# The decay's logits as one product over 96 rows of hi and lo parts, in place of an fp32 product over 32 rows

## The reference

```python
xn = _rmsnorm(x, p['norm1_g'])
z = jnp.einsum('btd,de->bte', xn, p['w_in'])
rg_x, rg_y, q, k, v, g_lr, g_out, m_a, m_b = jnp.split(z, split_points, axis=-1)
...
zg = jnp.einsum('btr,rk->btk', g_lr, p['gla_w_gate']) + p['gla_b_gate']
log_alpha = (jax.nn.log_sigmoid(zg.astype(f32)) / GLA_TAU).reshape(B, T, GLA_HEADS, GLA_DK)
```

## Time and profile before

| | |
|---|---|
| median of 3 runs | 1923.3 us (1923.18 to 1924.96) |
| the profiled execution, its own time | 1920.77 us |
| its span, first to last instruction | 1919.0 us |
| TensorE busy | 1890.9 us, 99% |
| weight loads on TensorE busy | 1860.3 us, 97% |
| VectorE busy | 921.1 us, 48% |
| ScalarE busy | 565.7 us, 29% |
| mean granted TensorE clock | 0.996 |

### The profile page before, as it was taken

One profiled execution on the slowest core, in us unless ns is written; L12 is line 12 of the kernel. 1 busy time (PEld: TensorE's weight loads), 2 busy tenths in 40 slices (PEclk: granted clock), 3 DMA queues, 4 the chain that ended last, 5 costly groups with the idle time before them and its releaser, 6 DMA issues. The chain is left out here.

```text
span 1919.0 us, 28820 instructions
## 1 busy us (share of the span) xinstructions
PE 1890.9 (99%) x11866; PEld 1860.3 (97%) x11866; DVE 921.1 (48%) x1067; ACT 565.7 (29%) x630; POOL 27.6 (1%) x24
## 2 busy tenths in 40 slices
PE   7999999999999999999999999999999999999998
PEld 6999899999999999999999999999999999999997
DVE  6221377788754222422244455545453545455455
ACT  5010256755642111211132332222121212131225
POOL 0000000000000000000000000000000000000032
PEclk9999999999999999999999999999999999999999
DMA  5221132223111111311131111111111111111112
GB/s 196 97 76 52 37 110 104 93 79 134 63 61 44 55 44 44 133 44 47 51 133 44 56 45 46 53 45 45 45 45 44 55 45 45 44 44 50 44 58 89
DMA packets 48234, 126.72 MB, mean 66 GB/s; under 512 B 7000, under 2 KB 20184, under 8 KB 48144
## 3 DMA queue, kind: packets, MB, share of 16 engines
q1 hardware_dynamic: 27808, 87.97, 13.6%
q10 hardware_dynamic: 20352, 37.64, 5.6%
HBM read 107.71 MB, written 18.14 MB: 66 GB/s over the span
## 5 line engine op out<-in xcount | busy, mean ns | idle before, releaser
L417 PE MATMUL acc<-xn_hi,w_hi 128*128 128x346 f32 (+1 forms) x2496 | 814.6, 326 | 2.5 <-issue 2.2
L417 PE MATMUL acc<-xn_lo,w_hi 128*128 128x346 f32 (+1 forms) x2496 | 803.6, 322 | 0.0
L417 PE MATMUL acc<-xn_hi,w_lo 128*128 128x346 f32 (+1 forms) x2496 | 801.5, 321 | 0.0
L417 PEld LDWEIGHTS acc<-xn_hi,w_hi 128*128 128x128 f32 x2496 | 470.9, 189 | 6.2 <-issue 3.4
L417 PEld LDWEIGHTS acc<-xn_lo,w_hi 128*128 128x128 f32 x2496 | 472.4, 189 | 1.5
L417 PEld LDWEIGHTS acc<-xn_hi,w_lo 128*128 128x128 f32 x2496 | 471.0, 189 | 0.0
L795 ACT ACTIVATE w_hi<-w_raw 128x1024 fp32r<-128x1024 f32 x149 | 156.4, 1050 | 460.2 <-PE acc L417 459.1
L1196 DVE TENSOR_TENSOR w_lo<-w_raw,w_hi 128x1024 fp32r<-128x1024 f32 x149 | 182.4, 1224 | 182.0 <-ACT w_hi L795 181.9
L417 PE MATMUL acc<-act_hi,w_hi 128*128 128x344 f32 x504 | 161.7, 321 | 2.6 <-DVE residual L1610 2.6
L417 PE MATMUL acc<-act_hi,w_lo 128*128 128x344 f32 x504 | 161.6, 321 | 0.0
L417 PE MATMUL acc<-act_lo,w_hi 128*128 128x344 f32 x504 | 161.6, 321 | 0.0
(11 more groups left out here) (229 smaller groups left out, 2209.2 us busy)
## 6 DMA issues: line engine op xcount, KB each, us to landing
w_raw<-in_w SPq DMA_DIRECT2D x152, 512.0 KB, 3.5
ha_scratch<-rg_gelu_ha ACTq DMA_DIRECT2D x8, 519.0 KB, 2.7
h<-ha_scratch ACTq DMA_DIRECT2D x8, 519.0 KB, 6.1
residual<-in_x ACTq DMA_DIRECT2D x8, 519.0 KB, 6.4
gla_qk_pair<-qk_scratch ACTq DMA_DIRECT2D x8, 512.0 KB, 4.5
smp_v_rows<-smp_v_scratch ACTq DMA_DIRECT2D x8, 512.0 KB, 5.7
out_gla_sample<-smp_state ACTq DMA_DIRECT2D x8, 512.0 KB, 3.1
smp_state<-in_gla_state ACTq DMA_DIRECT2D x7, 512.0 KB, 4.9
```

The lines of the kernel that those rows point to most:

```text
L417: mm = nc.tensor.matmul(acc[g][:, n, 0:cw], w[s][:, t * P:(t + 1) * P], x[:, c0 + n * cw:c0 + (n + 1) * cw], start=a, stop=z)
```

## The change

The low rank and the gate weights get hi and lo parts like the wide operands, and the three terms are laid on 96 rows of one product: rows 0 to 31 hold hi by hi, rows 32 to 63 lo values by hi weights, rows 64 to 95 hi values by lo weights. For that the low rank's 32 weight columns are written three times (`low4`), so that its products give 96 rows; the lo part of the inputs now goes through the same 96 columns. `wg` is loaded six times instead of twice. After the scaling, which now signals `low_scaled`, five ScalarE copies and two VectorE subtractions make the fp32r parts, in place and in two tiles that are free then (`low_t`, `wg_t`). `low_ready` has to reach 2.

```diff
-            for r in (0, RANK):
+            for r in range(0, R6, RANK):
                 sp.dma_start(wg[r:r + RANK, :], I["gla_w_gate"]).then_inc(const_loaded, 16)
...
-                    nc.tensor.matmul(acc[0][0:R2, n, 0:NW], whi[0][:, R2 * k:R2 * (k + 1)], XH[:, c], start=k == 0, stop=False)
-                    mm = nc.tensor.matmul(acc[0][0:RANK, n, 0:NW], whi[0][:, R2 * k:R2 * k + RANK], XL[:, c],
-                                          start=False, stop=k == KB - 1)
+                    w = whi[0][:, R6 * k:R6 * (k + 1)]
+                    nc.tensor.matmul(acc[0][0:R6, n, 0:NW], w, XH[:, c], start=k == 0, stop=False)
+                    mm = nc.tensor.matmul(acc[0][0:R6, n, 0:NW], w, XL[:, c], start=False, stop=k == KB - 1)
...
-                    mm = nc.tensor.matmul(sb6[:, h * w:(h + 1) * w], wg[0:R2, h * DK:(h + 1) * DK],
-                                          glr[0:R2, bass.ds(c0, w)], start=True, stop=True)
+                    mm = nc.tensor.matmul(sb6[:, h * w:(h + 1) * w], wg_s[0:R6, h * DK:(h + 1) * DK],
+                                          glr_s[0:R6, bass.ds(c0, w)], start=True, stop=True)
...
-                pe.wait_ge(const_loaded, 16 * 6)
-                pe.wait_ge(low_ready, 1)
+                pe.wait_ge(const_loaded, 16 * 10)
+                pe.wait_ge(low_ready, 2)
...
-                    nc.scalar.activation(view3(glr[0:R2]), acc[0][0:R2, :, 0:NW], ACT.Copy).then_inc(acc_free[0], 1)
+                    nc.scalar.activation(view3(glr[0:R6]), acc[0][0:R6, :, 0:NW], ACT.Copy).then_inc(acc_free[0], 1)
...
+            act.wait_ge(const_loaded, 16 * 10)
+            nc.scalar.activation(wg_s[0:2 * R2], wg[0:2 * R2], ACT.Copy).then_inc(wg_hi_done, 1)
+            nc.scalar.activation(wg_t[2 * R2:R6], wg[2 * R2:R6], ACT.Copy).then_inc(wg_hi_done, 1)
+            act.wait_ge(low_scaled, 1)
+            for r in (0, 2 * R2):
+                nc.scalar.activation(glr_s[r:r + R2], glr[r:r + R2], ACT.Copy).then_inc(low_hi_done, 1)
+            nc.scalar.activation(low_t[R2:2 * R2], glr[R2:2 * R2], ACT.Copy).then_inc(low_hi_done, 1)
...
-            nc.vector.tensor_tensor(low3[:, :, RANK:R2], hd(raw[0], KB, RANK), low3[:, :, 0:RANK].bitcast(F32), ALU.subtract)\
+            low = hd(raw[0], KB, RANK).unsqueeze(2).broadcast_to([P, KB, 3, RANK])
+            nc.vector.tensor_tensor(low4[:, :, :, RANK:R2], low, low4[:, :, :, 0:RANK].bitcast(F32), ALU.subtract)\
...
-            nc.vector.tensor_tensor(glr[0:R2, :], glr[0:R2, :], rms[0:R2, :], ALU.mult).then_inc(low_ready, 1)
+            nc.vector.tensor_tensor(glr[0:R6, :], glr[0:R6, :], rms[0:R6, :], ALU.mult).then_inc(low_scaled, 1)
...
+            dve.wait_ge(wg_hi_done, 2)
+            nc.vector.tensor_tensor(wg_s[2 * R2:R6], wg[2 * R2:R6], wg_t[2 * R2:R6].bitcast(F32), ALU.subtract).then_inc(low_ready, 1)
+            dve.wait_ge(low_hi_done, 3)
+            nc.vector.tensor_tensor(glr_s[R2:2 * R2], glr[R2:2 * R2], low_t[R2:2 * R2].bitcast(F32), ALU.subtract).then_inc(low_ready, 1)
```

More of the change, by code:

```diff
@@ L53 @@
 R2 = 2 * RANK
+R6 = 3 * R2
 CH = 64
@@ L149, in build @@
         it = nxt("rg_i_b", C)
+        av_at = off[0]
         av = nxt("rg_a", C)
+        th_at = off[0]
         th = nxt("rg_mult", C)
@@ L167, in build @@
         rgtmp = at("rg_states_tmp", qkp_at + 1024, KB * NS)
-        glr = nxt("gla_low_rank", C)
+        glr_at = off[0]
+        glr, glr_s = nxt("gla_low_rank", C), at("gla_low_rank_split", glr_at, C, F32R)
         gw = nxt("rg_gate_weights", 2 * P)
@@ L172, in build @@
         svt = svb
-        wg = nxt("gla_gate_weights", QK)
+        wg_at = off[0]
+        wg, wg_s = nxt("gla_gate_weights", QK), at("gla_gate_weights_split", wg_at, QK, F32R)
         reset = nxt("scan_reset", 4 * PAIR, BF16, 2)
@@ L204, in build @@
         sq1 = (rt, it, av, th)
+        low_t, wg_t = at("gla_low_rank_hi", av_at, C, F32R), at("gla_gate_weights_hi", th_at, QK, F32R)
         act_bytes = (2 * GRP * CB + 31) // 32 * 32
@@ L268, in build @@
         V3 = V.rearrange("p (k c) -> p k c", k=KB)
-        low_ready = sem("low_ready")
+        low_scaled, low_hi_done, wg_hi_done, low_ready = (sem(n) for n in ("low_scaled", "low_hi_done", "wg_hi_done", "low_ready"))
         w_loaded, w_hi_done, w_split, unit_done = sems("w_loaded"), sems("w_hi_done"), sems("w_split"), sems("unit_done")
@@ L559, in zg_samples @@
                 for h in range(H):
-                    mm = nc.tensor.matmul(sb6[:, h * NS:(h + 1) * NS], wg[0:R2, h * DK:(h + 1) * DK],
-                                          glr[0:R2, NT:C], start=True, stop=True)
+                    mm = nc.tensor.matmul(sb6[:, h * NS:(h + 1) * NS], wg_s[0:R6, h * DK:(h + 1) * DK],
+                                          glr_s[0:R6, NT:C], start=True, stop=True)
                 mm.then_inc(zg_mm, 1)
@@ L620, in zg_pair @@
                     for h in range(H):
-                        mm = nc.tensor.matmul(sb6[:, h * PAIR:(h + 1) * PAIR], wg[0:R2, h * DK:(h + 1) * DK],
-                                              glr[0:R2, bass.ds(NMETA + PAIR * j, PAIR)], start=True, stop=True)
+                        mm = nc.tensor.matmul(sb6[:, h * PAIR:(h + 1) * PAIR], wg_s[0:R6, h * DK:(h + 1) * DK],
+                                              glr_s[0:R6, bass.ds(NMETA + PAIR * j, PAIR)], start=True, stop=True)
                     mm.then_inc(zg_mm, 1)
@@ L813, in _ @@
             act.preload_act_table_set(LN_EXP)
-            low3 = whi[0][:, 0:KB * R2].rearrange("p (k r) -> p k r", k=KB)
+            low4 = whi[0][:, 0:KB * R6].rearrange("p (k t r) -> p k t r", k=KB, t=3)
             act.wait_ge(w_loaded[0], 16)
-            nc.scalar.activation(low3[:, :, 0:RANK], hd(raw[0], KB, RANK), ACT.Copy).then_inc(w_hi_done[0], 1)
+            low = hd(raw[0], KB, RANK).unsqueeze(2).broadcast_to([P, KB, 3, RANK])
+            nc.scalar.activation(low4[:, :, :, 0:RANK], low, ACT.Copy).then_inc(w_hi_done[0], 1)
             act.wait_ge(prm_loaded, 16)
@@ L1314, in scores @@
             def scores(n, w):
-                dve.wait_ge(const_loaded, 16 * 6)
+                dve.wait_ge(const_loaded, 16 * 10)
                 dve.wait_ge(A_mm, n + 1)
```

## The result

The changed kernel takes 1927.2 us (median of 11 runs, 1926.6 to 1929.2) against 1923.0 us of the kernel before beside it (11 runs): ratio 1.0027, 95% interval 1.0017 to 1.0036. It is slower by 4 to 5 us, a little more than can be told from no change, where no change was forecast. The profiled execution took 1927.11 us, with a span 6.3 us longer than that of the earlier trace rows.

What follows compares the result with a forecast made beforehand. TensorE, busy for 99% of the span, was taken as the bound; -7.1 us of products, +4.6 wait and +2.5 low clock summed to 0.0, so 1923.3 us, no change, with a range of 1919.6 to 1927.4.

Steps and rivals of the forecast that it cites:

- products, pair blocks: TensorE, eight pair blocks in the passes: four instructions at 0.11 us, each block 0.44 instead of 1.17 us; 5.8 us saved.
- products, head and samples: TensorE, the head's and the samples' logits blocks: each 0.44 instead of 1.08 us; 1.3 us saved.
- wait before the first logits: TensorE idles until ScalarE's copies and VectorE's last subtraction finish: 4.6 us, bounds 4.4 and 5.1.
- low clock behind it: After the idle time before the first logits, wide products come at 0.29 instead of 0.16 us; 2.5 us lost.
- given back in the passes: Passes over token pairs, 225 to 520 us: no wait that could take the saved time back; 0 us.
- The step that failed: Passes, 225 to 520 us: TensorE busy throughout, so each removed instruction shortens the span by its pitch, with no wait behind.
- One reading beside it: Around the first logits: ScalarE's table load, its next work, began long after the copies would end, so nothing gets late.
- fp32 pace with the fall: Rival: narrow products at 0.22 us each, plus wait and low clock; +3.5 us, 1926.8 us, chance 0.18.
- The hidden wait: Rival: before the first logits copies overlap more or run ahead, so the wait hardly shows; -7.1 us, 1916.2 us, chance 0.07.
- the clock that doesn't fall: Rival: same wait before the first logits, products behind it still at 0.16 us; -2.5 us, 1920.8 us, chance 0.23.
- a new wait of TensorE inside the passes: Sign named as making the prediction wrong; it expected no TensorE wait from 225 to 520 us.

Runs made afterwards that it cites:

- after_warm: Changed kernel with 32 unread wide products on TensorE ahead of its wait for the logits' inputs; 1923.0 us, ratio 0.9999 to the kernel before.
- early_split: Changed kernel with five ScalarE copies behind the q and k loop's first turn, two VectorE subtractions ahead of its other three; 1917.7 us, ratio 0.9972.
- early_chain: early_split with VectorE masking scores before scaling the unit into rg_ext and copying the output before the weight's lo part; 1913.6 us, ratio 0.9958.
- after_again: The changed kernel once more, unaltered, for a second profile; 1926.3 us in one run.
- pairs_fp32: Changed kernel with the eight pair blocks as plain fp32 products over rows 0 to 31, without the lo terms; 1931.0 us, ratio 1.0045.
- before_chain: Kernel before, products unchanged, with VectorE's scores ahead of the scaling and output copies ahead of the lo part; 1921.4 us, ratio 0.9989.
- before_scores: Kernel before with only VectorE's masking of the scores moved ahead of the scaling into rg_ext; 1923.2 us, ratio 1.0007.

## Why the prediction was wrong

| term, us | forecast | from the trace after |
|---|---|---|
| products, pair blocks | -5.8 | -6.2 |
| products, head and samples | -1.3 | -1.4 |
| late before the wait | 0 | 0.2 |
| wait before the first logits | 4.6 | 5.3 |
| low clock behind it | 2.5 | 2.6 |
| longer low clock near 220 us | not seen | 2.6 |
| given back in the passes | 0 | 3.7 |
| behind the passes | 0 | -0.5 |
| sum | 0.0 | 6.3 |

The 2.6 behind the wait is what the 6.65 us leave: 6.65 - 0.2 - 5.3 + 1.4. The second 2.6 is 9.3 - 6.65, 3.7 is 6.2 less the 2.5 that came back, and -0.5 is 6.3 - 6.8. The runs check them apart: 5.4 us for both clock terms (after_warm), 10.6 for wait and clock (early_split). For the passes early_split and early_chain do: the pair blocks take 264.3 and 260.3 us from first to last, and the medians, taken on two chips, lie 4.1 apart.

- **The step that failed** is the first one: "every instruction removed there shortens the span by its pitch, and no wait stands behind it that could take the time back". It was read from TensorE's 295.00 busy us of 295.00, which shows that TensorE waited for nothing there; it doesn't show by how much its inputs were ahead. VectorE's scores were only 0.35 us early, less than the 0.78 that a pass was to lose. Of the 6.2 us saved in the passes 3.7 went into a new wait and what follows it, and early_chain got them back.
- **The term that was missing** is the second low clock. The forecast took the fall behind the wait, rightly and at the right size, and took the fall of the earlier trace rows as given. It became twice as long, only in the kernels with the idle time (the changed kernel, after_again, pairs_fp32), and not in after_warm. The 2.6 hold for this pair of traces: before_chain and before_scores, which have the instructions of the kernel before up to there, had 3.4 and 10.2 us in place of 6.8, and the mean granted clock of the kernel before went from 0.994 to 0.998 in its runs beside the experiments, where all 11 of the changed kernel have 0.993. Against the median of the kernel before the term can be smaller, which fits medians that lie 4.2 apart and not 6.3.
- **The wait** was mis-sized: 5.3 where the bounds were 4.4 to 5.1. The place, the releaser and the in-order queue were right; the pitch of ScalarE's copies was that of copies of another shape and type. One reading beside it was wrong without a cost: ScalarE's table load began at 120.42 us, only 0.39 behind the reckoned end of the copies and not long after it; it now starts at 120.90, right behind the last copy, and TensorE doesn't wait for it.
- **The products** were right: (0.55 - 0.16) / 4 = 0.098 us each, where 0.11 was taken and 0.09 was the low end. The Trainium skill's four passes ("FP8 and Floating Point Precision", TensorE Precision Notes) made a block an estimate of 0.29 us; the trace has 0.39, a third of before and not a quarter.
- **The clock behind the wait** was what the Trainium skill warns of ("TensorE: Matmul & The Clock Gate", HAM oscillation), and the rows from 120 to 129 us now show a single gap within dense work doing it. On the later, longer fall the trace goes further than that sentence.
- **The rivals.** fp32 pace with the fall gave 1926.8, near the time that came, by a mechanism that was not there. Its nearness shows nothing: the distance of 0.55 us excludes it. The hidden wait is excluded by the 5.27 us, the clock that doesn't fall by the 0.50 of 122 to 127 us. That 1927.2 still lies inside the range is luck: its top, 1927.4, came from the fp32 pace.

The prediction named "a new wait of TensorE inside the passes" as what would make it wrong. That wait could have been found beforehand from the two rows of 319.59 and 320.70.

## What to carry to other kernels

Before a saving is counted in full on the busiest engine, look for the inputs that arrive just in time there: the end of the last producer against the start of its user is the slack, and a saving past it becomes a wait unless the producer's queue is put in order too. The slack tells that a wait will come, not what is kept: here it was 0.35 us, and once it was used up a pass kept about 0.1. Preparatory work for an engine that never stands still goes where its inputs first exist, not behind the loop that happens to end before its use. An idle time of TensorE costs more than its length: here 5.3 us of waiting cost another 5.4 at the low clock, half of it 100 us later.

## What the runs showed of the hardware

- Fp32r products of 96 rows and 128 moving columns follow each other at 0.098 us.
- ScalarE copies of 32 x 1050 into fp32r come at 1.10 us, those of 128 x 1050 into fp32 at 0.97; few partitions don't make them faster. Whether the shape or the type of the result makes the difference, no run separates.
- After one idle time of 5.3 us in dense work the clock is low once behind it and, 100 us of dense work later, falls earlier and for longer (13.6 instead of 6.8 us) in a step with few products. Why, stays open; with the same instructions up to there the kernel before, before_chain and before_scores had 6.8, 3.4 and 10.2 us, so its length varies without an idle time as well, but 13.6 was in no trace without one.
